# Hyena's filters made beside HGRN's last projections instead of beside the convolutions

## The chip, the cores and the metric

One NeuronCore of a Trainium2 chip runs the whole kernel, alone. The metric is the device time of one execution in microseconds (us), the median of the runs.

## The reference, cut to what matters

Two decoder blocks over 256 tokens of width 1024, all in float32. The change lies in the mixer of the second block, which joins two branches: HGRN (a gated linear recurrence in both directions) and Hyena (a long convolution whose filters a small network makes from positions).

```python
def hybrid_mixer(xn, w_in, ...):
    proj = xn @ w_in                       # q, zf_fwd, zf_bwd, inp, og, hy (3 x 1024), gates (2 x 1024)
    logf = log(lb + (1 - lb) * sigmoid(z)); k = (1 - lb) * sigmoid(-z)      # for z forward and backward
    o = scan(silu(q), k_f, logf_f, inp) + reversed scan(silu(q), k_b, logf_b, inp)
    y_a = (rmsnorm(o) * silu(og)) @ w_branch_a
    x0, x1, v = split(centred_short_conv(hy, conv_w, conv_b))                # width 3, along the tokens
    h_f, h_b = hyena_filters(...)
    y_b = (x0 * bidirectional_fftconv(v * x1, h_f, h_b, bias)) @ w_branch_b
    return (sigmoid(g_a) * y_a + sigmoid(g_b) * y_b) @ w_out

def hyena_filters(L, w1, b1, freq1, w2, b2, freq2, w3, decay_rate):
    z = concat([t, cos(ang), -sin(ang)])                # 256 x 33, constants
    hid = sin(freq1 * (z @ w1 + b1))                    # 256 x 64
    hid = sin(freq2 * (hid @ w2 + b2))                  # 256 x 64
    filt = (hid @ w3) * exp(-t * abs(decay_rate))       # 256 x 2048
    return filt[:, :1024], filt[:, 1024:]
```

The filters depend on weights and constants alone, on nothing that the input has gone through.

## The kernel before, in words

Activations lie transposed in SBUF, 128 channels a partition block, eight blocks of 256 tokens. A weight comes in units of 512 KB (128 x 1024 numbers) over SP's queue into a ring of 3 slots (`SLOTS`). A unit is used in one of two ways. `Whole` (L312) multiplies the float32 as it is: 8 matmuls, recorded as 16 instructions of line L402. `Split` (L334) lets ScalarE round a high part (L338), VectorE (L343) or GpSimd (L349) subtract a low part, into one of 3 buffers (`PARTS`), and multiplies in three passes, 24 matmuls of lines L370 to L372. A unit's product is one step, `Channels`; an "evac" behind it takes the result out of PSUM. `submit` fetches a unit now and plans its product two units later (`AHEAD = 2`).

A step is a small class with a method for each engine. The program is one list of steps, written by Python generators, and each engine goes through the same list in that order (`follow`), doing its own part of each step. Nothing is reordered at run time: an instruction that waits holds up all that stands behind it on its engine. A step with `phases = 3` stands three times in the list, and each time an engine runs to its next `yield`. `filler` generators supply projection units, one at each `next(filler)`, between the phases of other work. `Load` is a small transfer on SP's queue; `Barrier` drains the four compute engines and lets none pass until all have.

`second_mixer` does this, in order:

1. 16 units for the gates' logarithms and keys, with the norm.
2. `hgrn`: two logarithms, four scans, then nine `HgrnLevel`s in `pipeline(..., 2)`: two at a time, on PSUM banks 0 to 3. Each level makes operands (in `zf`, `zb` or in `hg_q2`, `hg_k2`) and the scores of 8 heads in two parts. Beside it the generator `more()` supplies units: q, v, `og`, gate_a and gate_b. It has 42 turns: 8 for q, 1, 8 for v, 1, and 8 each for og, gate_a and gate_b. `hgrn` yields 34 times (1 after the logarithms, 4 scans, 28 phases of levels and an empty turn), and these take 4 + 8 + 29 = 41 turns of `more()`.
3. `finish()`: the one turn left (it plans the product of gate_b's block 5), then `flush(w[32], w[40])`, which plans the products of blocks 6 and 7 and fetches the first two units of the convolutions. Then eight `HgrnHead`s (L2487 to L2494) and a barrier.
4. 24 projections with `ShortConv` behind them (L2796, L2803, L2806, L2810), 14 of their turns beside the `HeadNorm`s of 8 heads, and then 10 turns beside `filters`. A convolution's PSUM bank rotates over three, 4 to 6; it is free when VectorE is done with L2806.
5. `filters`: eight `Load`s (L293), `FilterDecay` (L2584), two `FilterLayer`s of two phases each (L2552 on TensorE, L2559 to L2569 on VectorE, the sine L2574 on ScalarE), and two `FilterTile`s of three phases each (exponential L2604, four matmuls of 512 columns recorded as 8 instructions L2611 into banks 0 to 3, and L2619 to L2625 on VectorE). The first layer's matmul waits for all eight loads; a tile's matmuls wait until VectorE has taken the tile before out of banks 0 to 3 (L2619).
6. A barrier, and then the transforms (`TurnU` L2709, `Transform` L2686), which read the filters.

Of the kernel before, what the change touches and what calls it, by code (L numbers as in the profile page):

```python
# [9 lines left out]
T, D, P = 256, 1024, 128  # L10
NT, KD = T // P, D // P
# [11 lines left out]
HG_H = 8  # L23
# [77 lines left out]
class Signal:  # L101
# [5 lines left out]
    def next(self):  # L107
        self.counted += self.by
        return Mark(self, self.counted)
# [71 lines left out]
def together(main, filler, every):  # L181

    for n, _ in enumerate(main):
        if n % every == 0:
            next(filler, None)
# [2315 lines left out]
def hgrn(c, ctx, s, q, zf, zb, bounded, v, o, finish):  # L2501


    logged = [c.plan(HgrnLogs(c, z[:, :, :], mark)).logged for z, mark in ((zf, bounded[0]), (zb, bounded[1]))]
    s.bf = c.sb("hg_bf", [P, HG_H, T], ctx)
    s.bb = c.sb("hg_bb", [P, HG_H, T], ctx)
    yield
    for back, (z, b) in enumerate(((zf, s.bf), (zb, s.bb))):
        for hd in range(0, HG_H, 4):
            s.scanned = c.plan(HgrnScan(c, z, b, range(hd, hd + 4), back, logged[back])).scanned  # L2510
            yield

    s.places = [(zf, zb), (c.sb("hg_q2", [P, HG_H, T], ctx), c.sb("hg_k2", [P, HG_H, T], ctx))]
    s.at = c.sb("hg_scores", [P, HG_H, NT, P], ctx)
    s.fwd = c.sb("hg_scores_fwd", [P, HG_H, P], ctx)
    s.bwd = c.sb("hg_scores_bwd", [P, HG_H, P], ctx)
    s.cleared = c.plan(HgrnClear(c, s.at[:, :, :, :], bounded[1])).cleared
    s.operands_free, s.kept = [(), ()], [None, None]

    yield from pipeline(c, [lambda u, n=n, m=m: HgrnLevel(c, s, n, m, u) for n, m in enumerate([P] + LEVELS + [0])], 2)  # L2520
    o_free = finish()
    for hd in range(HG_H):
        c.hg_taken = c.plan(HgrnHead(c, s, hd, v, o, o_free)).taken
        yield
# [105 lines left out]
    pass  # L2630


def filters(c, ctx, both):

    f = Filters()
    z = c.sb("filt_z", [EMB, T], ctx)
    w1 = c.sb("filt_w1", [EMB, FILT_H], ctx)
    w2 = c.sb("filt_w2", [FILT_H, FILT_H], ctx)
    f.w3 = c.sb("filt_w3", [FILT_H, 2 * D], ctx)
    vec = c.sb("filt_vec", [FILT_H, 4], ctx)  # L2640
    f.decay = c.sb("filt_decay", [P, 2 * D], ctx)
    f.window = c.sb("filt_window", [P, 2 * D], ctx)
    f.cols = c.sb("filt_cols", [P, 2 * NT], ctx)
    f.hid = c.sb("filt_hid", [FILT_H, T], ctx)
    turns = c.sb("filt_turns", [FILT_H, T], ctx)
    f.came = [c.load(z[:, :], c.dram["filter_z"]), c.load(w1[:, :], c.dram["filt_w1_2"]),
              c.load(w2[:, :], c.dram["filt_w2_2"]), c.load(f.w3[:, :], c.dram["filt_w3_2"]),
              c.load(vec[:, :], c.dram["filt_vec"]),
              c.load(f.decay[:, :], c.dram["filt_decay_2"].partition_broadcast(P)),
              c.load(f.cols[:, 0:NT], c.dram["minus_t"]), c.load(f.cols[:, NT:2 * NT], c.dram["not_first"])]  # L2650
    f.decay_ready = c.plan(FilterDecay(c, f.decay[:, :], f.came)).ready
    ready = f.came
    for n, (w, x) in enumerate(((w1, z), (w2, f.hid))):
        layer = FilterLayer(c, w[:, :], x[:, :], ready, f.hid[:, :], turns[:, :], vec[:, 2 * n:2 * n + 1],
                            vec[:, 2 * n + 1:2 * n + 2])
        ready = list(f.came) + [layer.ready]
        for _ in range(layer.phases):
            c.plan(layer)
            yield
    f.window_free = ()  # L2660
    for i in range(NT):
        tile = FilterTile(c, f, i, layer.ready, both)
        for _ in range(tile.phases):
            c.plan(tile)
            yield
    c.filters_made = tile.made
# [179 lines left out]
def second_mixer(c, h, xn, work, gained, make_norm, following):  # L2846

    w = c.dram["w_in_2"]
    with ExitStack() as ctx:
# [2 lines left out]
        og = c.sb("hg_og", [P, KD, T], ctx)  # L2852
        sga = c.sb("gate_a", [P, KD, T], ctx)
        sgb = c.sb("gate_b", [P, KD, T], ctx)
        o = work
        with ExitStack() as inner:
            q = c.sb("hg_q", [P, HG_H, T], inner)
            zf = c.sb("hg_zf", [P, HG_H, T], inner)
            zb = c.sb("hg_zb", [P, HG_H, T], inner)
            v = c.sb("hg_v", [P, NT, D], inner)  # L2860
            z = [zf[:, n, :] for n in range(KD)] + [zb[:, n, :] for n in range(KD)]
            s = Hgrn()
            s.q = q
            s.kf = c.sb("hg_kf", [P, HG_H, T], inner)
            s.kb = c.sb("hg_kb", [P, HG_H, T], inner)
            k = [s.kf[:, n, :] for n in range(KD)] + [s.kb[:, n, :] for n in range(KD)]
            keys = []

# [45 lines left out]
            filler = in_turns(more())  # L2914

            def finish():
                for _ in filler:
                    pass
                c.whole = False
                c.low_by = "pool"  # L2920
                c.flush(w[32], w[40])
                return xn.whole_free

            for n, _ in enumerate(hgrn(c, inner, s, q, zf, zb, bounded, v, o, finish)):
                for _ in range(4 if n == 0 else 2 if 4 < n < 9 else 1):
                    next(filler, None)
            gated_ready, gates_ready = gates
            c.barrier()
        both = c.sb("filters", [P, NT, 2, D], ctx)
        with ExitStack() as inner:  # L2930
            sq = c.sb("hg_sq", [P, HG_H, T], inner)
            tmps = c.sb("hg_tmp", [P, 2, T], inner)
            x = c.sb("hy_x", [P, T], inner)
            lent = []

            def convolved():
                for n in range(KD):
                    c.channels(w[32 + n], xn, ShortConv(c, n, x0[:, n, :]))
                    yield
                    c.channels(w[40 + n], xn, ShortConv(c, 8 + n, u[:, n, :]))  # L2940
                    yield
                    c.channels(w[48 + n], xn, ShortConv(c, 16 + n, x[:, :], u[:, n, :], lent))
                    yield

            filler = convolved()
            heads, tmps_free = [], [(), ()]

            def head(b, hd):
                norm = HeadNorm(c, o, hd, b, sq, tmps, tmps_free, c.gain("hgrn_norm_g_2"), og, [c.hg_taken, gated_ready])
                heads.append(norm.normed)  # L2950
                return norm

            next(filler)
            next(filler)
            next(filler)
            together(pipeline(c, [lambda b, hd=hd: head(b, hd) for hd in range(HG_H)], 2), filler, 2)
            together(filters(c, inner, both), filler, 1)
            for _ in filler:
                pass
            c.low_by = "vector"  # L2960
            c.flush(c.dram["w_branch_a_2"][0], c.dram["w_branch_a_2"][1])
            u_ready = c.last_conv
            c.barrier()
# [282 lines left out]
```

## Time and profile before

| what | value |
|---|---|
| median of 3 runs | 2531.92 us (2531.15 to 2541.61) |
| the profiled execution's own time | 2539.18 us |
| its span, from first to last instruction | 2537.4 us |
| TensorE busy / VectorE / ScalarE / GpSimd | 94% / 65% / 53% / 31% |
| granted TensorE clock, mean | 0.966 |

Times inside the span are in us from its start. An engine's busy share says little alone here: what counts is who is late at each place. PE is TensorE's matmul row, DVE VectorE, ACT ScalarE, POOL GpSimd, SPq SP's queue of transfers. The clock is given as a share of 2.4 GHz: 1.00 is that, 0.50 is 1.2 GHz.

### The profile page before, as it was taken

How to read it: one execution, taken by the hardware profiler on the slowest of the kernel's cores; microseconds unless marked ns; L12 is line 12 of the kernel's file. 1: busy time of each engine (PE TensorE's matmuls, PEld its weight loads, DVE VectorE, ACT ScalarE, POOL GpSimd, SP SyncE). 2: the span in 40 equal slices, each digit the busy share in tenths (PEclk: the TensorE clock that was granted, in tenths of full speed). 3: DMA queues.
4: the chain of work that ended last, by engine and by line, in shares of the span. 5: the costliest groups of instructions: out<-in, count | busy, mean ns of one | idle time of the engine just before them, and what ended most of it. 6: DMA issues, size and time to landing. Idle time of an engine off the chain costs nothing.

```text
span 2537.4 us, 39066 instructions
## 1 busy us (share of the span) xinstructions
PE 2375.6 (94%) x15354; PEld 2140.5 (84%) x15354; DVE 1660.1 (65%) x3193; ACT 1343.1 (53%) x2494; POOL 775.4 (31%) x404
## 2 busy tenths in 40 slices
PE   6878898999999999998888988899999999999998
PEld 5876788999999888886857976799999999788886
DVE  4564456977777556665667384666977778555555
ACT  3345344468887454444433444244468888444443
POOL 3000002877776000000800152101877777000000
PEclk8888899999999999999999998999999999999999
DMA  5322234555555656664332342254555555565563
GB/s 172 124 95 69 92 100 149 176 176 165 165 164 170 185 191 192 192 192 128 125 116 93 116 148 95 67 165 151 183 175 166 162 164 169 180 189 186 189 187 120
DMA packets 108287, 383.36 MB, mean 151 GB/s; under 512 B 12976, under 2 KB 15841, under 8 KB 107529
## 3 DMA queue, kind: packets, MB, share of 16 engines
q1 hardware_dynamic: 108104, 380.86, 47.3%
q8 instruction: 123, 2.02, 0.3%
q14 instruction: 60, 0.48, 0.1%
HBM read 379.74 MB, written 1.06 MB: 150 GB/s over the span
## 4 chain that ended last, share of the span: by engine, by line
PE 81%; DVE 11%; ACT 4%; DMA 2%; issue 2%; POOL 0%; SPq 0%; DVEq 0%; ACTq 0%; POOLq 0%
PE psum L370 23%; PE psum L372 22%; PE psum L371 22%; PE psum L2021 2%; PE psum L402 2%; DVE weight_parts L343 2%; ACT weight_parts L338 2%; PE psum L607 1%; PE psum L2466 1%; PE psum L2686 1%; PE psum L1457 1%; PE psum L1018 1%; PE psum L1357 0%; DVE hg_tmp L1064 0%; PE psum L2611 0%
## 5 line engine op out<-in xcount | busy, mean ns | idle before, releaser
L349 POOL TENSOR_TENSOR weight_parts<-weight_ring,weight_parts 128x1024 fp32r<-128x1024 f32 x276 | 670.8, 2442 | 506.5 <-ACT weight_parts L338 506.0
L370 PE MATMUL psum<-acts_high,weight_parts 128*128 128x256 f32 x2744 | 794.1, 289 | 23.4 <-DVE weight_parts L343 11.2
L338 ACT ACTIVATE weight_parts<-weight_ring 128x1024 fp32r<-128x1024 f32 x674 | 710.6, 1055 | 150.1 <-PE psum L372 79.2
L372 PE MATMUL psum<-acts_high,weight_parts 128*128 128x256 f32 x2744 | 782.6, 285 | 0.0
L371 PE MATMUL psum<-acts_low,weight_parts 128*128 128x256 f32 x2744 | 782.1, 285 | 0.0
L343 DVE TENSOR_TENSOR weight_parts<-weight_ring,weight_parts 128x1024 fp32r<-128x1024 f32 x398 | 488.4, 1228 | 296.1 <-ACT weight_parts L338 295.5
L370 PEld LDWEIGHTS psum<-acts_high,weight_parts 128*128 128x128 f32 x2744 | 532.1, 194 | 34.6 <-issue 12.5
L371 PEld LDWEIGHTS psum<-acts_low,weight_parts 128*128 128x128 f32 x2744 | 532.4, 194 | 1.4 <-issue 0.5
L372 PEld LDWEIGHTS psum<-acts_high,weight_parts 128*128 128x128 f32 x2744 | 532.4, 194 | 0.0
L370 PE MATMUL psum<-weight_parts,peer_coef 128*128 128x512 f32 x1024 | 405.9, 396 | 4.0 <-issue 3.9
L372 PE MATMUL psum<-weight_parts,peer_coef 128*128 128x512 f32 x1024 | 404.8, 395 | 0.0
L371 PE MATMUL psum<-weight_parts,peer_coef 128*128 128x512 f32 x1024 | 402.8, 393 | 0.0
L2103 ACT ACTIVATE peer_coef<-peer_experts 128x256 fp32r<-128x256 f32 x256 | 106.8, 418 | 356.5 <-PE psum L372 355.4
L370 PEld LDWEIGHTS psum<-weight_parts,peer_coef 128*128 128x128 f32 x1024 | 193.4, 189 | 46.5 <-issue 4.2
L372 PEld LDWEIGHTS psum<-weight_parts,peer_coef 128*128 128x128 f32 x1024 | 193.3, 189 | 45.3
L371 PEld LDWEIGHTS psum<-weight_parts,peer_coef 128*128 128x128 f32 x1024 | 193.2, 189 | 44.3
L2107 DVE TENSOR_TENSOR peer_coef<-peer_experts,peer_coef 128x256 fp32r<-128x256 f32 x256 | 108.5, 425 | 153.6 <-ACT peer_coef L2103 153.6
L2002 ACT ACTIVATE peer_second_keys<-psum,work 128x128 fp32r<-128x128 f32 x512 | 146.2, 371 | 14.9 <-DVE peer_second_keys L1993 13.7
L585 POOL TENSOR_TENSOR work<-h 128x256 f32<-128x256 f32 x32 | 19.4, 614 | 410.7 <-DVE h L569 399.5
L2082 ACT ACTIVATE peer_experts<-psum 128x256 f32<-128x256 f32 (+35 forms) x250 | 78.2, 313 | 121.1 <-PE psum L372 121.0
L1990 DVE TENSOR_TENSOR psum<-psum,work 128x512 f32<-128x512 f32 x128 | 89.2, 697 | 59.7 <-ACT peer_second_keys L2002 58.6
L370 PE MATMUL psum<-acts_spare_high,weight_parts 128*128 128x256 f32 x352 | 103.2, 293 | 16.9 <-DVE weight_parts L343 16.8
(426 smaller groups left out, 3135.4 us busy)
## 6 DMA issues: line engine op xcount, KB each, us to landing
weight_ring<-in_peer_down SPq DMA_DIRECT2D x128, 512.0 KB, 3.6
weight_ring<-in_peer_up SPq DMA_DIRECT2D x128, 512.0 KB, 3.5
weight_ring<-in_peer_u SPq DMA_DIRECT2D x128, 512.0 KB, 3.6
weight_ring<-in_peer_v SPq DMA_DIRECT2D x128, 512.0 KB, 3.5
weight_ring<-in_w_in SPq DMA_DIRECT2D x88, 512.0 KB, 3.6
weight_ring<-in_w_out SPq DMA_DIRECT2D x16, 512.0 KB, 3.6
weight_ring<-in_peer_w_q SPq DMA_DIRECT2D x16, 512.0 KB, 3.6
weight_ring<-in_w_in_v SPq DMA_DIRECT2D x10, 512.0 KB, 3.6
```

The costliest lines, as they stand in the source:

```text
L338: q.e.activation(self.high, self.ring, ACT.Copy).then_inc(*self.rounded.once())
L343: q.e.tensor_tensor(self.low, self.ring, self.high.bitcast(F32), ALU.subtract).then_inc(*self.unit.ready.once())
L349: q.e.tensor_tensor(self.low, self.ring, self.high.bitcast(F32), ALU.subtract).then_inc(*self.unit.ready.once())
L370: q.e.matmul(out, sh, mh, start=first, stop=False)
L371: q.e.matmul(out, sh, ml, start=False, stop=False)
L372: return q.e.matmul(out, sl, mh, start=False, stop=last)
L402: last = q.e.matmul(self.out, w[:, k, :], acts.whole[:, k, :], start=k == 0, stop=k == KD - 1)
L1990: q.e.tensor_tensor(ones, iota, over(x.pairs[:, 1, tokens], P, 2), ALU.is_equal).then_inc(*self.marked.once())
L2002: last = q.e.activation(self.second[:, t, 1, :], self.c.bank(6)[:, P * t:P * t + P], ACT.Copy, bias=0.0, scale=x.gates_low[:, token:token ...
L2082: last = q.e.activation(self.x.experts[:, self.n, n:T], out[:, n:T], ACT.Gelu_apprx_tanh)
L2103: q.e.activation(self.high, self.src, ACT.Copy).then_inc(*self.rounded.once())
L2107: q.e.tensor_tensor(self.low, self.src, self.high.bitcast(F32), ALU.subtract).then_inc(*self.ready.once())
```

## The change

The place in the order changes: `filters` is started in `finish()`, right behind the levels, instead of behind the head norms. Its first turn comes ahead of the last turn of `more()`, its second behind it, and the rest follow at once, ahead of the flush that plans the last two products. The tiles `hg_kf`, `hg_kb`, `hg_q2`, `hg_k2` now lie in a stack of their own (`levels`) which is closed there, and the filters' tiles take that space; so the eight loads wait for the last scores of the last two levels (`s.operands_free`). The result, `both`, lies open from the mixer's start, and `hg_bf`, `hg_bb` are views of it, since the filters are written only when the levels are through. Behind the head norms the call of `filters` goes, and the ten convolution turns that went beside it follow one another.

```diff
-    s.bf = c.sb("hg_bf", [P, HG_H, T], ctx)
-    s.bb = c.sb("hg_bb", [P, HG_H, T], ctx)
...
-    s.at = c.sb("hg_scores", [P, HG_H, NT, P], ctx)
-    s.fwd = c.sb("hg_scores_fwd", [P, HG_H, P], ctx)
-    s.bwd = c.sb("hg_scores_bwd", [P, HG_H, P], ctx)
...
-def filters(c, ctx, both):
+def filters(c, ctx, both, after):
...
-    f.came = [c.load(z[:, :], c.dram["filter_z"]), c.load(w1[:, :], c.dram["filt_w1_2"]),
...
+    f.came = [c.load(out, src, after) for out, src in (
+        (z[:, :], c.dram["filter_z"]), (w1[:, :], c.dram["filt_w1_2"]), (w2[:, :], c.dram["filt_w2_2"]),
+        (f.w3[:, :], c.dram["filt_w3_2"]), (vec[:, :], c.dram["filt_vec"]),
+        (f.decay[:, :], c.dram["filt_decay_2"].partition_broadcast(P)), (f.cols[:, 0:NT], c.dram["minus_t"]),
+        (f.cols[:, NT:2 * NT], c.dram["not_first"]))]
...
+        both = c.sb("filters", [P, NT, 2, D], ctx)
...
-            s.kf = c.sb("hg_kf", [P, HG_H, T], inner)
-            s.kb = c.sb("hg_kb", [P, HG_H, T], inner)
+            s.bf, s.bb = (both[:, i, :, :].rearrange("p a d -> p (a d)").rearrange("p (h t) -> p h t", h=HG_H)
+                          for i in range(NT))
+            s.at = c.sb("hg_scores", [P, HG_H, NT, P], inner)
+            s.fwd = c.sb("hg_scores_fwd", [P, HG_H, P], inner)
+            s.bwd = c.sb("hg_scores_bwd", [P, HG_H, P], inner)
+            levels = inner.enter_context(ExitStack())
+            s.kf = c.sb("hg_kf", [P, HG_H, T], levels)
+            s.kb = c.sb("hg_kb", [P, HG_H, T], levels)
...
             def finish():
+                levels.close()
+                made = filters(c, inner, both, s.operands_free[0] + s.operands_free[1])
+                next(made)
                 for _ in filler:
+                    next(made, None)
+                for _ in made:
                     pass
                 c.whole = False
                 c.low_by = "pool"
                 c.flush(w[32], w[40])
                 return xn.whole_free
 
-            for n, _ in enumerate(hgrn(c, inner, s, q, zf, zb, bounded, v, o, finish)):
+            for n, _ in enumerate(hgrn(c, levels, s, q, zf, zb, bounded, v, o, finish)):
...
-        both = c.sb("filters", [P, NT, 2, D], ctx)
...
             together(pipeline(c, [lambda b, hd=hd: head(b, hd) for hd in range(HG_H)], 2), filler, 2)
-            together(filters(c, inner, both), filler, 1)
             for _ in filler:
                 pass
```

## Rows read from the trace of the kernel before

**Rows 1.** Page, part 1: busy us (share of the span) x instructions.
```profile
PE 2375.6 (94%) x15354; PEld 2140.5 (84%) x15354; DVE 1660.1 (65%) x3193; ACT 1343.1 (53%) x2494; POOL 775.4 (31%) x404
```
**Rows 2.** Stretches, TensorE alone: length, busy (x), granted clock, DMA share, GB/s.
```profile
1454.90:1501.00 46.10, 40.48 (x304) 0.96 0.46 141
1501.00:1559.80 58.80, 50.49 (x308) 0.85 0.34 106
1559.80:1564.20 4.40, 0.04 (x1) 0.84 0.00 0
```
**Rows 3.** TensorE's waits, 1430 to 1640: us in total, times, longest.
```profile
PE psum L2552 <- ACT filt_hid L2574: 4.8, 1, 4.8
PE psum L2709 <- DVEq L816: 4.4, 1, 4.4
```
**Rows 4.** TensorE in order of time: start, us, instruction, [idle before <- releaser].
```profile
1426.33 0.27 PE L2466 MATMUL psum<-hg_q,hg_zb 128*128 128x128 f32 x1
...
1437.32 0.38 PE L402 MATMUL psum<-work,weight_ring 128*128 128x256 f32 x1
...
1447.10 0.27 PE L2487 MATMUL psum<-hg_scores,hg_v 128*128 128x128 f32 x1
...
1502.75 0.61 PE L2552 MATMUL psum<-filt_z,filt_w 33*64 33x256 f32 x2 [1.76 <-DMA filt_cols<-in_not_first]
```
**Rows 5.** SP's queue in order of time: start, us of issuing.
```profile
1434.64 0.33 SPq L334 DMA_DIRECT2D weight_ring<-in_w_in  x1
...
1491.92 0.31 SPq L293 DMA_DIRECT2D filt_z<-in_filter_z  x1
...
1495.66 0.42 SPq L293 DMA_DIRECT2D filt_cols<-in_not_first  x1
```
**Rows 6.** Transfers issued 1486 to 1512: KB, us from issue to landing.
```profile
filt_cols<-in_not_first SPq DMA_DIRECT2D x1, 1.0 KB, 6.9
```
**Rows 7.** The chain that ended last, 1240 to 1640: start, us, what.
```profile
1443.81 3.46 PE psum L402 x16
...
1514.16 1.11 PE psum L2552 x2
...
1524.28 6.26 PE psum L2611 x8
...
1541.55 3.63 PE psum L2611 x8
```
**Rows 8.** ScalarE in order of time.
```profile
1440.97 0.39 ACT L537 ACTIVATE gate_b<-psum 128x256 f32<-128x256 f32 x1 [1.34 <-PE psum L402]
...
1525.08 0.55 ACT L2796 ACTIVATE hy_x<-psum,gains 128x256 f32<-128x256 f32 x1
1525.64 1.28 ACT L2604 ACT_TABLE_LOAD   x1
1526.94 2.00 ACT L2604 ACTIVATE filt_window<-filt_decay,filt_cols 128x2048 f32<-128x2048 f32 x1
```
**Rows 9.** VectorE in order of time.
```profile
1508.66 0.48 DVE L2806 SCALAR_TENSOR_TENSOR hy_x<-psum,gains,hy_x 128x255 f32<-128x255 f32 x1
...
1509.58 0.54 DVE L2559 TENSOR_SCALAR filt_hid<-psum,filt_vec 64x256 f32<-64x256 f32 x1
...
1513.37 0.28 DVE L2569 TENSOR_SCALAR filt_hid<-filt_hid 64x256 f32<-64x256 f32 x1
```
**Rows 10.** Groups by line, 1501 to 1564: xcount, busy us, mean ns, idle before.
```profile
L2619 DVE TENSOR_TENSOR filt_window<-filt_window,psum 128x2048 f32<-128x2048 f32 x2 | 4.6, 2276 | 0.0
...
L2574 ACT ACTIVATE filt_hid<-filt_hid 64x256 f32<-64x256 f32 x2 | 0.8, 416 | 8.8 <-DVE filt_hid L2569 8.8
```
**Rows 11.** Stretches, TensorE alone (columns as in Rows 2).
```profile
1514.10:1518.20 4.10, 4.04 (x16) 0.50 0.00 0
...
1524.20:1535.40 11.20, 11.12 (x31) 0.55 0.32 94
...
1545.10:1559.70 14.60, 14.60 (x121) 1.00 0.30 88
```

More of the change, by code:

```diff
@@ L2645, in filters @@
     turns = c.sb("filt_turns", [FILT_H, T], ctx)
-    f.came = [c.load(z[:, :], c.dram["filter_z"]), c.load(w1[:, :], c.dram["filt_w1_2"]),
[L2647 to L2650, printed above, removed]
+    f.came = [c.load(out, src, after) for out, src in (
[3 more added lines that the diff above has]
+        (f.cols[:, NT:2 * NT], c.dram["not_first"]))]
     f.decay_ready = c.plan(FilterDecay(c, f.decay[:, :], f.came)).ready
```

## The prediction

> **What bounds the kernel now.** The page comes first: TensorE is busy 94% of the span, nobody else over 65% [rows 1]. So an edit pays where it takes away time in which TensorE stands still or runs at the lower clock, and costs where it adds such time. The stretches show both states side by side [rows 2]. In the last stretch of the convolutions (1501.0 to 1559.8) 12 projections of 24 matmuls pass in 58.8 us, with TensorE busy 50.5 us at a mean clock of 0.85. Further on, where the filters' TensorE work is done, five such projections take 14.6 us, 2.9 us each [rows 11]. Twelve at that pace are 34.8 us, so the filters take 24.0 us of TensorE's time there. The list of waits and the order of time name the pieces: 1.8 us for the filters' loads [rows 4], 4.8 us for the first sine [rows 3], 4.1 us of the low clock after it [rows 11], 6.3 and 3.6 us of matmuls for the two tiles [rows 7], and nearly 11 us more of the low clock around the first of them [rows 11]. After the last convolution TensorE waits another 4.4 us for the barrier [rows 2, 3], because VectorE is late there.
>
> The new place has to be read as closely. There, between the levels' last scores (1426.33) and the first head (1447.10), TensorE runs six projections without a gap [rows 4]. Nothing is idle there to be filled on TensorE.
>
> **What the change takes away.** (a) The filters' 24.0 us between 1501.0 and 1559.8. The cover that they leave must be counted. In the fast cadence the third of the 12 projections would start at 1501.0 + 2 x 2.9 = 1506.8. It needs the bank of the third before it, which VectorE, busy with the last two head norms, frees at 1508.66 + 0.48 = 1509.1 [rows 9]. Today that lateness hides behind the filters; then it costs 2.3 us. Bounds: 0, if VectorE gets there sooner, to 4.6, if the low clock follows. I take 2.3. (b) The 4.4 us before the barrier. Without the filters' last instructions ahead of it VectorE needs for the last projection only the evac on ScalarE (0.55 [rows 8]), twice 0.48 [rows 9] and a product of about as much, some 2.1 us. It gains 2.3 us. Together 24.0 - 2.3 + 2.3 = 24.0 us, between 20 and 26.5. The eight transfers and ScalarE's decay that go from here hide behind projections today and gain nothing more.
>
> **What it adds.** The step list says who stands behind whom. `more()` has one turn left when `finish()` starts, so the order on TensorE becomes: gate_b's block 4, the first layer's matmul, block 5, the second layer's matmul, tile 0, tile 1, blocks 6 and 7, the heads. One projection, block 5, lies between two links of the chain; blocks 6 and 7 and the 32 heads' matmuls are ready and stand behind the whole of it. So the filters' latency is laid open almost entirely:
>
> - *The loads.* Their wait for the levels' scores costs nothing: the scores start at 1426.33 [rows 4], and SP gets there when it has issued the transfer at 1434.64 [rows 5]. The last of the eight is issued 3.7 us after the first (1491.92 to 1495.66) and lands 6.9 us on [rows 5, 6]: 1435.0 + 3.7 + 6.9 = 1445.6. TensorE has finished block 4 by 1437.5 (block 5 begins at 1437.32 today [rows 4]) and stands still for about 8 us. Bounds: landing 2 us sooner or later, since two weight units shared the wires today and about as much does then. The weight unit of block 7 is issued 4 us later, behind the loads; its product comes 30 us later, so that is free.
> - *First layer, block 5.* The matmul takes 0.6 [rows 4], to 1446.2. Block 5 takes 3.5 us at the full clock (rows of block 7, [rows 7]); after a stand of 4.8 us the low clock lasted for 4.1 us of work [rows 3, 11], so I take 5.3: 1451.5. The bounds are 3.5 and 6.9.
> - *To the second sine.* VectorE's part of a layer lasts from 1509.58 to 1513.65, 4.1 us, with two convolution instructions of 0.48 in it [rows 9]: 3.1 us net, done by 1449.5, while block 5 runs. But ScalarE has the evac of block 5 ahead of the sine: 0.4 [rows 8], then the table for the sine, 1.3 (as the load at 1525.64 [rows 8]), and the sine, 0.4 [rows 10]: 1453.6. Second layer: matmul 1.1 [rows 7], VectorE 3.1, sine 0.4: 1458.2.
> - *Tile 0.* 6.3 us at the low clock, 3.6 at the full one [rows 7]. It follows a stand of 3.5 us on one of 2, so I take 6.3: 1464.5. The exponential (1.3 and 2.0 [rows 8]) lies beside it. Then L2619, 2.3 us [rows 10], on which tile 1's matmuls wait: 1466.8.
> - *Tile 1.* Between 3.6 and 6.3; I take 5.0: 1471.8. Blocks 6 and 7 start here, at first perhaps at the low clock: 1 us more, with 0 and 2.3 as bounds. Tile 1's work on VectorE ends beside them, before the heads need the banks.
>
> Today block 6 starts at 1437.32 + 3.5 = 1440.8. The place gets longer by 1471.8 + 1.0 - 1440.8 = 32.0 us. With everything at the full clock and the loads 2 us early it is 23; with everything at the low clock and the loads 2 us late, 37.
>
> **A rule weighed.** ScalarE's row shows a table load of 1.28 us between an instruction that ends at 1525.63 and one that starts at 1526.94, with nothing else in the gap [rows 8]. The Trainium skill (ScalarE: Activation LUTs, "What ACT_TABLE_LOAD costs") adds a drain of 1.38 us to every switch of tables. By that rule the sine's switch on the open chain would cost 2.7 instead of 1.3 and the place 33.4 instead of 32.0. The trace does not agree: there is no room for it between the two instructions.
>
> **The sum.** 32.0 - 24.0 = 8 us longer. Against the profiled execution's own 2539.18 that is 2547; it is 7.3 above the median shown, so for the median 2531.9 + 8 = 2540.
>
> **The rivals.**
>
> *The low clock lasts through the whole chain.* One mechanism, in the new place: TensorE gets nothing long enough to do to be granted the full clock between 1441 and block 7. For it: around tile 0 today the clock was low for most of 11.2 us although projections ran [rows 11]; in the new place it has less to do. Against it: after the stand of 4.8 us it was low for only 4.1 us [rows 11]. Price over mine: block 5 6.9 (+1.6), tile 1 6.3 (+1.3), blocks 6 and 7 (+1.3), and the low clock behind the third convolution's wait (+2.3): 14.5 us in sum, 2546. From 12.7 us on it counts as slower, so two or three of these pieces decide.
>
> *The two places cancel.* The full clock returns in each gap and the loads come 2 us early: 23 to 27 against 24, 2532 to 2535. For it: tile 1 took only 3.6 us today [rows 7]. Against it: that tile came after 10 us of unbroken work, and here each piece has a stand of 2 to 8 us ahead.
>
> *The chain is hidden, as the words of the change have it.* If the projections did run beside the filters, only the filters' own matmuls would be added, 0.6 + 0.6 + 3.6 + 3.6 = 8.4 us, against 24.0 saved: 15.6 us faster, 2516. For it: the filters need nothing of TensorE but these 20 matmul records. Against it is the order of the step list: one turn is left, and each engine keeps its order. The 4.8 us before the second layer's matmul [rows 3] show that TensorE does wait with projections ready behind it.
>
> **How the numbers follow.** A measurement of this kernel can tell about 0.5%, 12.7 us, from no change. The sum as forecast 0.50, the low clock's rival 0.30, the two places cancelling 0.16, the hidden chain 0.04. The sum and the cancelling lie within 0.5% (0.66), the low clock beyond it (0.30), the hidden chain is faster (0.04). The range: below, 23 - 26.5 = -3, 2529; above, 37 - 20 = 17 us, 2549, and 3 us more for the spread of the runs: 2552. The hidden chain and half of what lies beyond 2552 stay outside.
>
> **What would show it.** In the profile after: TensorE idle for about 8 us ahead of L2552, released by the load of `not_first`; idle some 2 and 3.5 us ahead of the second L2552 and the first L2611, released by the sine; the first head 30 to 35 us later than 1447.1; a granted clock near 0.5 over most of it; the 12 last convolutions in about 37 us, with one gap of some 2 us; and the barrier's wait at 2 instead of 4.4. The prediction is wrong if projections run between the links of the chain, if the loads land far from 10.6 us after the first issue, or if the last 12 convolutions keep a pace above 3.1 us each.

## The result, and the profile after

After: 2549.97 us (median of 9 runs, 2544.02 to 2555.59). Before, on the same chip: 2535.14 us (9 runs, 2531.09 to 2541.61). The ratio is 1.006, with a 95% interval of 1.0049 to 1.0071, so the change costs 12.4 to 18.0 us. The profiled execution after took 2550.1 us, with a span of 2548.3 and a mean granted clock of 0.963.

The page's first part shows nothing of it. TensorE's busy time stands at 2376.0 against 2375.6 [rows 1]:

```profile
PE 2376.0 (93%) x15354; PEld 2141.6 (84%) x15354; DVE 1663.5 (65%) x3193; ACT 1342.8 (53%) x2494; POOL 770.9 (30%) x404
```

I cut both executions at the same instructions, and take the length of each piece (us):

| piece | before | after | difference |
|---|---|---|---|
| start to the levels' first score | 1294.0 | 1299.9 | +5.9 |
| the levels, first to last score | 134.0 | 135.8 | +1.8 |
| **last score to first head (the new place)** | 18.9 | 55.4 | **+36.5** |
| first head to first evac of a convolution | 11.2 | 11.2 | 0 |
| **first to last evac of the convolutions** | 101.7 | 79.6 | **-22.1** |
| last evac to `TurnU`'s first matmul (barrier) | 4.3 | 2.3 | -2.0 |
| from there to the first transform | 5.5 | 6.3 | +0.8 |
| first transform to the end | 967.8 | 957.8 | -10.0 |

The four pieces that the change can reach from the last score on give +36.5 - 22.1 - 2.0 + 0.8 = +13.2 us. The first and the last piece run the same code in both kernels. Over all the profiled executions of this document the first took 1288 to 1308 us and the last 958 to 968, whatever the kernel. One profile against one can't tell that apart, which is why I compare pieces below and not spans.

The stretches of the new place, TensorE alone (columns as in [rows 2]); the last three are the convolutions and the barrier, which answer to [rows 2]:

```profile
1445.20:1453.20 8.00, 0.01 (x1) 0.81 0.85 270
1453.20:1459.30 6.10, 6.07 (x18) 0.68 0.01 3
1459.30:1465.80 6.50, 0.68 (x3) 0.85 0.46 161
1465.80:1482.70 16.90, 14.37 (x17) 0.50 0.00 1
1482.70:1488.00 5.30, 5.30 (x26) 0.52 0.00 0
1499.10:1543.70 44.60, 38.99 (x304) 1.00 0.38 119
1543.70:1581.90 38.20, 36.30 (x288) 0.96 0.48 152
1581.90:1584.20 2.30, 0.00 (x0) 1.00 0.00 0
```

TensorE stands for 8 us, works for 6, stands again for nearly all of 6.5, and then runs for 22 us (two tiles with one more stand of 2.4 between them, and block 6) at the low level of its clock (0.50 and 0.52, so 1.2 GHz). What it waits for there (us in total, times, longest):

```profile
PE psum L2547 <- DMA filt_cols<-in_not_first: 8.0, 1, 8.0
...
PE psum L2606 <- ACT filt_hid L2569: 3.7, 1, 3.7
...
PE psum L2606 <- DVE filt_window L2614: 2.4, 1, 2.4
PE psum L2705 <- DVEq L816: 2.3, 1, 2.3
PE psum L2547 <- ACT filt_hid L2569: 2.2, 1, 2.2
```

The lines are 5 lower than before: L2547 is a layer's matmul (before L2552), L2606 a tile's (L2611), L2569 the sine, L2614 the first product of a tile. Four of the rows are the chain's own links, 16.3 us; the fifth is the barrier's wait, 2.3 instead of 4.4 [rows 3]. The chain that ended last runs through the same instructions:

```profile
1446.54 6.45 DMA filt_cols<-in_not_first
1453.23 1.08 PE psum L2547 x2
1454.31 5.04 PE psum L402 x16
1459.77 1.28 ACT L2569
1461.07 0.42 ACT filt_hid L2569
1461.54 0.66 PE psum L2547 x2
...
1465.88 7.21 PE psum L2606 x8
1473.18 2.30 DVE filt_window L2614
1475.53 7.19 PE psum L2606 x8
```

One projection, block 5 (L402), lies between two links; all the others come ahead of the chain or behind it. The eight instructions of a tile took 7.21 and 7.19 us here, 6.26 and 3.63 before [rows 7].

### The profile page after: what moved, and what is told of

Same layout as the page of the kernel before. It is cut to its first block, busy times and chain, and to the rows that moved or that the text cites. A ratio compares the mean times of both kernels' runs of the same rounds, so it can differ in the third digit from the quotient of the medians.

```text
span 2548.3 us, 39060 instructions
## 1 busy us (share of the span) xinstructions
PE 2376.0 (93%) x15354; PEld 2141.6 (84%) x15354; DVE 1663.5 (65%) x3193; ACT 1342.8 (53%) x2494; POOL 770.9 (30%) x404
## 4 chain that ended last, share of the span: by engine, by line
PE 77%; DVE 15%; ACT 4%; DMA 2%; issue 2%; SPq 0%; POOL 0%; DVEq 0%; ACTq 0%; POOLq 0%
PE psum L370 22%; PE psum L372 21%; PE psum L371 21%; PE psum L2021 2%; PE psum L402 2%; DVE weight_parts L343 2%; ACT weight_parts L338 1%; PE psum L607 1%; PE psum L2466 1%; PE psum L2682 1%; PE psum L1457 1%; PE psum L1018 1%; DVE peer_experts L1887 1%; DVE peer_experts L1879 1%; DVE peer_experts L1881 1%
## 5 line engine op out<-in xcount | busy, mean ns | idle before, releaser
L338 ACT ACTIVATE weight_parts<-weight_ring 128x1024 fp32r<-128x1024 f32 x674 | 710.8, 1055 | 143.0 <-PE psum L372 81.6
```

The lines of the kernel that those rows point to most:

```text
L338: q.e.activation(self.high, self.ring, ACT.Copy).then_inc(*self.rounded.once())
```

## The experiments

All times are medians with the ratio to the kernel before on the same chip. "The place" is the piece from last score to first head: 18.9 us before, 55.4 after. `e1` to `e4` were measured beside a before of 2537.23, `e5` to `e7` of 2535.18, `e8` and `e9` of 2536.5, `e10` and `e11` of 2541.59. Where the chain ends right ahead of the heads, the low clock behind it falls on the heads, which the place leaves out: from first head to first evac it is 13.4 us in e4, 13.1 in e7, 12.9 in e9 and 12.2 in e8, against 11.2 before and after.

| | median | ratio [95%] | levels | place | convolutions |
|---|---|---|---|---|---|
| e1 loads early | 2542.73 | 1.0025 [1.0006, 1.0045] | 138.5 | 45.7 | 79.6 |
| e2 none | 2508.78 | 0.9878 [0.9854, 0.9902] | 135.9 | 18.9 | 79.0 |
| e3 warm | 2537.02 | 1.0002 [0.9989, 1.0016] | 132.9 | 44.5 | 79.6 |
| e4 blocks first | 2552.09 | 1.0057 [1.0032, 1.0081] | 137.8 | 54.4 | 78.9 |
| e5 woven | 2541.04 | 1.0024 [1.0003, 1.0045] | 143.6 | 38.2 | 78.9 |
| e6 spread | 2549.57 | 1.0052 [1.0026, 1.0079] | 134.2 | 18.9 | 118.2 |
| e7 fetch first | 2545.03 | 1.0035 [1.0016, 1.0053] | 137.8 | 51.7 | 79.0 |
| e8 woven behind | 2528.70 | 0.9980 [0.9960, 1.0000] | 138.5 | 32.1 | 78.9 |
| e9 order alone | 2535.20 | 0.9994 [0.9975, 1.0013] | 138.8 | 35.3 | 79.1 |
| e10 woven around | 2521.33 | 0.9919 [0.9890, 0.9947] | 137.8 | 29.6 | 79.0 |
| e11 burst | 2526.56 | 0.9947 [0.9923, 0.9971] | 139.7 | 29.6 | 79.2 |

**e2_none.** The filters are left out altogether; the transforms read whatever lies in `both`. What do they cost in each place?

```diff
-                made = filters(c, inner, both, s.operands_free[0] + s.operands_free[1])
-                next(made)
                 for _ in filler:
-                    next(made, None)
-                for _ in made:
                     pass
+                c.filters_made = None
```

> The changed kernel with the filters left out altogether (no loads, layers, tiles; the transforms read what HGRN left in that space, so the output isn't the reference's). It measures both sides of the sum at once. Theory 1: the place shrinks from 44.2 us later than before to 7.7 later in the profiled pair, so 36.5 us go: 2550 - 36.5 = 2513, 22 below the kernel before. Rival (the convolutions ran slowly before for another reason than the filters beside them): less than 15 below the kernel before, 2520 or more.

The place is 18.9 us, as before, and the convolutions take 79.0. So after's 36.5 us in the place are the filters' whole, and before they cost 101.7 - 79.0 = 22.7 between the convolutions and 2.1 at the barrier, near the 24.0 that I had read off. By the pieces this kernel is 24.6 us shorter than before, by the medians 28.4 (interval 24.9 to 37.0). No edit accounts for the rest; it stays open.

**e1_loads_early.** The eight loads are planned ahead of gate_a's units, into tiles laid out before the levels' or views of `x0` and `u`, which are free there. Nothing else moves.

```diff
...
+                load_filters(c, f, [c.last_kept])
                 for n in range(KD):
                     c.channels(w[56 + n], xn, Keep(sga[:, n, :]))
...
-                made = filters(c, inner, both, s.operands_free[0] + s.operands_free[1])
+                made = filters(c, inner, both, f)
```

> The changed kernel, with the filters' eight loads issued in the middle of HGRN's levels, behind og's projections (w3 lies in the space of hy_x0, decay in that of hy_u, both unused until the convolutions). Theory 1 (the place costs the sum of the chain's latencies, laid open by the order of the steps): the stand of 8.0 us ahead of the first layer's matmul goes, and with it the low clock in block 5 (5.1 instead of 3.5 us): 9.6 us less than the changed kernel, 2540. The tiles stay at 7.2 us each. Rival (something else of the place binds, such as ScalarE behind block 5, and the stand only moves on): the second layer's matmul comes no earlier than 4 us before, 2546 or more.

The place is 9.7 us shorter. The stand of 8.0 us is gone, and with it the low clock of the first layer and block 5; the other links and the low clock from the first tile to block 6 are as they were. TensorE's waits, and the whole stretch from the first layer to block 7:

```profile
PE psum L2606 <- ACT filt_hid L2569: 3.7, 1, 3.7
PE psum L2606 <- DVE filt_window L2614: 2.5, 1, 2.5
PE psum L2547 <- ACT filt_hid L2569: 2.3, 1, 2.3
```
```profile
1447.40:1484.00 36.60, 28.12 (x79) 0.67 0.12 43
```

**e3_warm.** After, with 34 spare matmuls (17, 4, 8 and 5) into a bank of no use ahead of the chain's links. They add work and change nothing else, so they separate the clock from the waits.

```diff
+                c.plan(Dummies(c, 17))
                 next(made)
                 for _ in filler:
                     next(made, None)
+                c.plan(Dummies(c, 4))
+                next(made)
+                next(made)
+                c.plan(Dummies(c, 8))
...
+                c.plan(Dummies(c, 5))
```

> The changed kernel with 34 matmuls more, of the ones by a constant tile into PSUM bank 7, read by nobody: 17 ahead of the first layer's matmul, 4 ahead of the second, 8 ahead of tile 0, 5 ahead of tile 1, about as long at the full clock (0.43 us each) as TensorE stands still in each place. It takes the low clock away and leaves every latency. Theory 1: block 5 loses 1.6 us, the tiles 3.6 each, block 6 2.4 and the first layer 0.5: 11 us less than the changed kernel, 2539, still above the kernel before. Rival (the low clock is the main cost of the place): over 20 us less, below 2530.

The clock is 1.00 through the whole stretch, and the place is 10.9 us shorter with more work in it. That prices the low clock:

```profile
1442.50:1477.90 35.40, 33.83 (x146) 1.00 0.29 93
```

The kernel is back at the time of before (1.0002). By the pieces: 36.5 - 10.9 for the place, -22.1 for the convolutions, -2.0 and +0.3 around the barrier give +1.8.

**e4_blocks_first.** Blocks 5, 6 and 7 go ahead of the filters; only the loads are planned before them.

```diff
+    yield
     f.decay_ready = c.plan(FilterDecay(c, f.decay[:, :], f.came)).ready
...
                 for _ in filler:
-                    next(made, None)
-                for _ in made:
                     pass
                 c.whole = False
                 c.low_by = "pool"
                 c.flush(w[32], w[40])
+                for _ in made:
+                    pass
```

> The changed kernel, with the loads issued where they are, but blocks 5, 6 and 7 of gate_b planned ahead of the first layer, so that their 10 us lie beside the landing of the loads; the chain then stands alone, ahead of the heads. Theory 1: the stand of 8.0 us is covered and ScalarE has no evac ahead of the sine; the chain still costs 0.6 + 3.6 + 1.1 + 3.6 + 7.2 + 2.4 + 7.2 us, the heads wait 2.4 us more for tile 1's L2614 and start at the low clock: 6 to 8 us less than the changed kernel, 2543. Rival (projections between the links matter more than the landing): no gain, 2550.

A miss by 9 us: the place is 54.4. The loads stand ahead of block 7's weight unit on SP's queue, and TensorE now waits for that unit instead of for `not_first`; and with no projection left between them the links are as bare as before. The filters' last work also moved in front of the heads (L2487):

```profile
PE psum L402 <- DMA weight_ring<-in_w_in: 4.6, 1, 4.6
PE psum L2547 <- ACT filt_hid L2569: 3.7, 1, 3.7
PE psum L2606 <- ACT filt_hid L2569: 3.7, 1, 3.7
PE psum L2487 <- DVE filt_window L2614: 2.5, 1, 2.5
```

**e7_fetch_first.** Like e4, but the loads too are planned behind the fetch of block 7's weight unit.

```diff
+    yield
     f.decay_ready = c.plan(FilterDecay(c, f.decay[:, :], f.came)).ready
...
-                next(made)
                 for _ in filler:
-                    next(made, None)
-                for _ in made:
                     pass
+                next(made)
                 c.whole = False
                 c.low_by = "pool"
                 c.flush(w[32], w[40])
+                for _ in made:
+                    pass
```

> e4_blocks_first with the weights of block 7 fetched ahead of the filters' eight loads instead of behind them. In e4_blocks_first TensorE stood 4.6 us for them, and block 7 then took 6.0 us at the low clock. Theory 1: both go, 7 us less than e4_blocks_first, the place 47 instead of 54.4 us, 2545. Rival (the covered landing of the filters' loads is now the wait): the place no shorter than 52.

The time came out as expected, but the place is 51.7 and not 47. The stand of 8.0 is gone, and 7.8 us came at the second layer. ScalarE's rounding of a convolution's weight unit (L338) is ahead of the sine on its queue and waits 6.44 us for that unit. It lands late: the two units issued behind the loads took 7.2 us from issue to landing (median), against 3.7 for the units around the place before:

```profile
PE psum L2547 <- ACT filt_hid L2569: 7.8, 1, 7.8
```
```profile
1446.57 1.06 ACT L338 ACTIVATE weight_parts<-weight_ring 128x1024 fp32r<-128x1024 f32 x1 [6.44 <-DMA weight_ring<-in_w_in]
```

After, e4 and e7 together: a burst of loads at the time of use costs 4 to 8 us wherever it is put (8.0 in after, 4.6 in e4, 7.8 instead of e4's 3.7 at the second layer in e7). e1, whose loads are issued by 1373.7, 74 us ahead of the first layer, is rid of it.

**e5_woven.** e1, with both layers beside the last phases of the levels, the tiles among the last blocks. The layers use PSUM bank 7, which the levels leave free.

```diff
-        self.bias, self.freq, self.b = bias, freq, 3
+        self.bias, self.freq, self.b = bias, freq, 7
...
+                if n == 29:
+                    made = filters(c, inner, both, f)
+                if 29 < n < 34:
+                    next(made)
...
+                next(made)
+                next(made)
+                next(made)
                 c.whole = False
                 c.low_by = "pool"
-                c.flush(w[32], w[40])
+                c.prepared.append(c.fetch(w[32]))
+                c.work_off()
+                for _ in made:
+                    pass
+                c.flush(w[40])
```

> The filters in the new place, woven so that a projection stands between every two links: loads early as in e1_loads_early; the two layers on PSUM bank 7, their four turns beside the last level's phases (blocks 2 to 4 between them); tile 0 ahead of block 5, tile 1 ahead of block 6, block 7 and the heads behind. Theory 1: only the filters' own matmuls stay on TensorE, 0.6 + 0.6 + 3.6 + 3.6 = 8.4 us at the full clock and a little waiting: the place is 18.9 + 9 to 12 instead of 55.4 us, the convolutions stay as short as in the changed kernel; 2537 - 24 + 11 = 2524, about 13 below the kernel before. Rival (ScalarE, with two more table switches among gate_b's evacs, binds instead): place over 40, 2535 or more.

A miss by 17 us. The place fell to 38.2, but the levels rose to 143.6. Projections did lie between the links; now each link stood behind something else on its own engine. TensorE's waits, and what ScalarE did:

```profile
PE psum L2606 <- ACT filt_hid L2569: 4.7, 1, 4.7
PE psum L2466 <- DVE hg_scores L2435: 2.6, 1, 2.6
```
```profile
1455.42 1.06 ACT L338 ACTIVATE weight_parts<-weight_ring 128x1024 fp32r<-128x1024 f32 x1 [3.20 <-DMA weight_ring<-in_w_in]
```

A level's scores waited for a copy behind the filters' work on VectorE, and the tile's matmuls for a sine behind a weight unit that had not landed.

**e6_spread.** The other side: the kernel before, with its filters not behind but among the head norms, where the convolutions run anyway.

```diff
+    yield
     f.decay_ready = c.plan(FilterDecay(c, f.decay[:, :], f.came)).ready
...
-            together(pipeline(c, [lambda b, hd=hd: head(b, hd) for hd in range(HG_H)], 2), filler, 2)
-            together(filters(c, inner, both), filler, 1)
+            made = filters(c, inner, both)
+            next(made)
+            for n, _ in enumerate(pipeline(c, [lambda b, hd=hd: head(b, hd) for hd in range(HG_H)], 2)):
+                if n % 2 == 0:
+                    next(filler, None)
+                if n in (10, 13, 16, 19):
+                    next(made)
+            for n, _ in enumerate(made):
+                next(filler, None)
+                if n in (0, 3):
+                    next(filler, None)
```

> The kernel before, the filters at their old place, but with the loads at the stage's start, the four turns of the layers beside the head norms, three of their phases apart, and the tiles' six turns beside eight of the last ten convolutions' turns. Theory 1 (what the filters cost there was latency with too few projections between the links, and the place as such is not at fault): the waits of 1.8, 4.8 and 1.7 us and half of the low clock go, 12 us below the kernel before, 2525. Rival (VectorE, which carries the head norms, passes the layers' 6 us on to TensorE): 5 or less below, 2532.

A miss by 25 us: the convolutions take 118.2 instead of 101.7. There VectorE is the late one, and the filters' instructions are put in its way: a head norm's sum waits 7.9 us, since its square stands behind the first sine on ScalarE, and the sine waits for VectorE. The loads at the head of the stage delay the weights: the two units issued right behind them took 8.0 us to land (median), and ScalarE waits 7.52 us:

```profile
PE psum L1050 <- ACT hg_sq L1040: 9.2, 3, 7.9
PE psum L2611 <- ACT filt_hid L2574: 6.9, 1, 6.9
PE psum L370 <- POOL weight_parts L349: 6.2, 2, 5.7
```
```profile
1466.56 1.06 ACT L338 ACTIVATE weight_parts<-weight_ring 128x1024 fp32r<-128x1024 f32 x1 [7.52 <-DMA weight_ring<-in_w_in]
```

**e9_order_alone** and **e8_woven_behind.** e1's loads; behind the levels the blocks 5, 6 and 7 are dealt out, one between two links (`work_off` plans a product that has been fetched). e8 adds three things: gate_b's sigmoid is taken off the blocks' evacs and done later in one instruction, so ScalarE changes its table less; the heads use banks 4 to 7, so that they needn't wait for the filters' last product; and `flush(w[32])` goes ahead of the tiles' last part. The edit of e9:

```diff
                 made = filters(c, inner, both, f)
                 next(made)
+                next(made)
                 for _ in filler:
-                    next(made, None)
+                    pass
+                next(made)
+                next(made)
+                c.work_off()
+                next(made)
+                c.work_off()
                 for _ in made:
                     pass
```

and what e8 has besides:

```diff
-        self.b = hd % 4
+        self.b = (7, 4, 5, 6)[hd % 4]
...
-                    c.channels(w[64 + n], xn, Keep(sgb[:, n, :], ACT.Sigmoid))
+                    c.channels(w[64 + n], xn, Keep(sgb[:, n, :]))
...
-                c.flush(w[32], w[40])
+                c.flush(w[32])
+                for _ in made:
+                    pass
+                c.flush(w[40])
...
+        gate_b_ready = c.plan(Activate(c, sgb[:, :, :], ACT.Sigmoid, gate_b_kept)).ready
```

> e1_loads_early with nothing changed but the order in finish(): both turns of the first layer, block 5, both of the second, block 6, tile 0's matmuls, block 7, then the rest. e5_woven moved three things at once and put links behind weights that were still landing and behind VectorE's parts of the last level; here the levels are left alone and no weight is fetched between the links. Theory 1: TensorE's row from block 4 to the first head is 0.6 + 3.5 + 0.6 + 3.1 + 0.5 + 3.6 + 3.5 + 3.6 us and 2.6 for the heads' wait on tile 1's L2614, 21.6 where the kernel before has 10: place 30 instead of e1_loads_early's 45.7 us, 2526, 11 below the kernel before. Rival (a chain between short projections stays open, since ScalarE serves evac, sine and tables in one row): place 38 or more, 2533.

> e9_order_alone, and beside it tile 0's part on VectorE and tile 1's matmuls behind block 7 as there, but the heads on PSUM banks 7, 4, 5 and 6 instead of 0 to 3, so that they don't wait for tile 1, and gate_b kept plain out of PSUM, with one sigmoid over all of it much later, so that no table is switched between the links. Theory 1: the heads' wait of 2.6 us goes: place 28, 2523, 14 below the kernel before. Rival (the wait only moves on to the barrier behind the heads, or the later sigmoid costs as much): equal to e9_order_alone within 1 us of the sum of the stretches.

e9 came 9 us above its expectation, with a place of 35.3 instead of 30; e8 with 32.1 instead of 28. Of the waits, 6.9 us are left in e9:

```profile
PE psum L2487 <- DVE filt_window L2614: 3.8, 1, 3.8
PE psum L2547 <- ACT filt_hid L2569: 2.5, 1, 2.5
PE psum L2606 <- ACT filt_hid L2569: 0.6, 1, 0.6
```

The order is the larger step, 45.7 to 35.3; e8's three edits give 3.2 more together, and 0.8 in the heads. They were not run apart.

**e10_woven_around** and **e11_burst.** The first layer goes into the levels' last phase (turn 33), where the levels' own work is over, the second among the blocks; gate_b's sigmoid is late, as in e8, and the loads go out one by one beside the units of `og`. e11 is e10 with the loads in one burst ahead of gate_a's units, as in e1.

```diff
+                if n == 33:
+                    made = filters(c, inner, both, f)
+                    next(made)
+                    next(made)
+                    c.work_off()
+                    next(made)
+                    next(made)
...
                 for _ in filler:
-                    next(made, None)
+                    pass
+                next(made)
+                c.work_off()
+                next(made)
+                next(made)
+                next(made)
+                c.work_off()
```

and from e10 to e11:

```diff
                     c.channels(w[24 + n], xn, Keep(og[:, n, :]))
-                    if n == 0:
-                        loads = load_filters(c, f, [c.last_kept])
-                    next(loads)
                     yield
+                load_filters(c, f, [c.last_kept])
                 for n in range(KD):
                     c.channels(w[56 + n], xn, Keep(sga[:, n, :]))
```

> The links of the chain one projection further forward than in e8_woven_behind, each with its successor one projection away and no link behind a weight that still lands: first layer (both turns), block 4, second layer (both turns), block 5, tile 0's matmuls, block 6, tile 0's rest and tile 1's matmuls, block 7, tile 1's rest, heads on banks 0 to 3 as before; the fetch of block 6's weights comes behind the second layer. The eight loads go out one at a time beside og's eight projections. gate_b plain, with the late sigmoid. Theory 1: the filters' own 8.4 us on TensorE and nothing else: place 27 to 28 us (18.9 before, 32.1 in e8_woven_behind), 14 us below the kernel before by the stretches, 2522. Rival (another queue takes over again: VectorE's or ScalarE's weight parts): place over 31.

> e10_woven_around with its eight loads in one burst behind og's projections, as in e1, e8 and e9, whose levels took 138.5 to 138.8 us where they took 134.0 before. If the burst of 1.5 MB makes the weights of gate_a late, the levels take 138 us here and 134 in e10_woven_around, and 4 us stand between the two; if those 4 us are the clock's own spread between executions, the two kernels agree within 2 us.

e10 beats both kernels: 0.9919 of before, 20 us less (interval 13 to 28). The whole place runs at the full clock, and the links' waits sum to under 1 us:

```profile
1428.90:1455.30 26.40, 25.59 (x118) 1.00 0.25 80
```
```profile
PE psum L2547 <- ACT filt_hid L2569: 0.7, 1, 0.7
...
PE psum L2487 <- DVE filt_window L2614: 0.2, 1, 0.2
```

Its place is 29.6 us (27 to 28 were expected), 10.7 above before; that is the filters' own matmuls, 8.4 us, and 2 us. By the pieces from the last score on it is 14 us shorter than before, with the levels' +3.8 it is 10; the medians say 13 to 28, so they are kinder than the one profile. The place of e11 is the same 29.6. Neither outcome of its expectation came: its levels took 139.7 us against 137.8, and the medians stand 5 us apart. The two ratios' intervals overlap: that the burst costs anything there is not shown.

## Why the prediction came out as it did

The forecast was +8 us, 2540; what came was about +15, 2550. That lies inside the range but outside the forecast's own "within 0.5%". The first rival, the low clock that lasts, came nearer with its +14.5 (2546; both sums were counted from the 2531.92 shown, and before's nine runs have 2535.14). Step by step, with after's times brought to before's scale (this execution reached the place 7.7 us later):

- **The order, and the chain laid open: right.** TensorE's queue shows it as forecast, and the rival that hides the chain fell.
- **The loads: right.** A stand of 8.0 us for `not_first`, as forecast. e1 gives it back, 9.7 us in the place.
- **First layer, block 5, second sine: right.** Block 5 ended within 0.2 us of the forecast and tile 0 began within 0.1. The rival had block 5 at 6.9; it took 5.04. The clock had fallen during the stand of 8.0 us and came back inside block 5, at 1457.0; it was at 0.50 again from the stand ahead of tile 0 until the end of block 6:

```profile
1450.20:1457.00 6.80, 3.77 (x9) 0.50 0.36 141
1457.00:1463.80 6.80, 2.98 (x13) 1.00 0.44 154
1464.00:1487.70 23.70, 19.37 (x39) 0.50 0.00 1
```

- **Tile 0: 6.3 forecast, 7.2 measured.** The row of 6.26 [rows 7] was taken for a tile at the low clock; it was one in which the clock fell on the way. Before, TensorE passed the tile's first us at 0.99 and the rest at 0.50 (the 0.55 over the stretch [rows 11] holds both):

```profile
1524.28:1525.28 1.00, 1.00 (x3) 0.99 0.00 0
1525.30:1530.54 5.24, 5.24 (x8) 0.50 0.33 97
```

  A tile all at 0.50 takes 7.2, twice the 3.63 of full speed.
- **Tile 1: 5.0 forecast, 7.2 measured.** Here the sum failed most, by 2.2 us. I took a value inside bounds of 3.6 and 6.3, and the upper one was too low as well. Behind the stand of 3.7 the clock stayed at 0.50 through both tiles, with 7.2 us of unbroken work on either side of the stand of 2.4.
- **Block 6: +1.0 forecast, +2.4 measured.** Its 24 matmuls passed at a mean of 0.52.
- These three make 0.9 + 2.2 + 1.4 = 4.5 us, and the place came out at +36.5 instead of +32.0. e3 shows the cause: with the clock held at 1.00 the same place is 10.9 us shorter, and the sum had 6.9 us of low clock in it (1.8 in block 5, 2.7 and 1.4 in the tiles, 1.0 in block 6). The step that was mis-sized is the price of the low clock in the tiles and block 6, whose mechanism I had and whose size I split with its rival. The upper bound was added up wrongly too: with everything at the low clock and the loads 2 us late the terms give 38.2, not 37.
- **The gain: 24.0 forecast, 23.3 measured; the sum is near, its parts came otherwise.** Convolutions -22.1, barrier -2.0, transforms +0.8. Of the 22.1, 1.5 came ahead of the filters' old place (46.1 to 44.6 us at clocks of 0.96 [rows 2] and 1.00), which the sum did not have. The last 12 convolutions took 38.2 us where it had 37.1. That is 3.18 us each, just past the 3.1 which the prediction had set as a sign of being wrong. The wait of 2.3 for the third product's bank did not come. In its place the first product of the stretch waited 1.89 us for GpSimd's low part and then ran at the low clock; the stretch ended 3.4 us above the fast pace:

```profile
1545.58 0.42 PE L370 MATMUL psum<-acts_high,weight_parts 128*128 128x256 f32 x1 [1.89 <-POOL weight_parts L349]
```

- **The table rule of the Trainium skill (ScalarE: Activation LUTs, "What ACT_TABLE_LOAD costs"): not borne out, as forecast.** ScalarE's rows of after show the load and the sine behind it with 0.02 us between them, as before; there is no drain of 1.38 us. The measurement decides here: a switch costs 1.3 us.

```profile
1459.37 0.38 ACT L537 ACTIVATE gate_b<-psum 128x256 f32<-128x256 f32 x1 [4.37 <-PE psum L402]
1459.77 1.28 ACT L2569 ACT_TABLE_LOAD   x1
1461.07 0.42 ACT L2569 ACTIVATE filt_hid<-filt_hid 64x256 f32<-64x256 f32 x1
```

The pieces give +13.2, the medians +12.4 to +18.0. That both are past +8 is shown; the 2 us between them are not explained.

The levels took 134 us in before and e6, 133 to 136 in after, e2 and e3, 137.8 to 138.8 in e1, e4, e7, e8, e9 and e10, 139.7 in e11 and 143.6 in e5. They go with the granted clock inside them: 0.95, 0.94, 0.93, 0.91 and 0.92 in that order. e4 and e7 have their loads late and stand with the slower ones, so the traces do not show that early loads slow the levels. Why the clock differs there is open.

## What to carry to other kernels

In these runs a dependent chain of short pieces was hidden only where the in-order list itself had independent work between every two links, on every engine that the chain passes (e10). Moving it "beside" such work left it bare, and then the stands were paid twice, as waits and as the low clock that came with them (here 16 us and 11 us). Ahead of such a move, look at each engine's queue for what stands before the link, above all an instruction that waits for a weight still on its way; and issue the chain's loads a stage early.

## What the runs showed of the hardware that was not expected

- A tile's eight matmul instructions took 7.2 us at a granted clock of 0.50 and 3.63 at 1.00 [rows 7]; 34 spare matmuls, which hold the clock, made the place shorter by 10.9 us.
- Unbroken work did not keep the clock up or bring it back at once. Before, it fell 1 us into tile 0, behind a stand of 1.7 us, and stayed at 0.50 for the rest of the tile. After, it stayed at 0.50 from 1464.0 to 1487.7 although TensorE was busy for 19.37 of these 23.7 us, the last 12 of them without a gap. Why is open.
- VectorE slows beside GpSimd. In e9 the same sum of the filters, two inputs in SBUF, took 1.23 us while GpSimd was idle and 3.27 when GpSimd was making low parts beside it; the next of the kind, which began at 1470.12, after GpSimd's end at 1469.10, took 1.21. The first fence is VectorE's, the second GpSimd's:

```profile
1458.56 1.23 DVE L2619 TENSOR_TENSOR filters<-filt_window 128x1024 f32<-128x1024 f32 x1
...
1466.93 3.27 DVE L2619 TENSOR_TENSOR filters<-filt_window 128x1024 f32<-128x1024 f32 x1
```
```profile
1463.98 5.12 POOL L349 TENSOR_TENSOR weight_parts<-weight_ring,weight_parts 128x1024 fp32r<-128x1024 f32 x2 [204.35 <-ACT weight_parts L338]
```

The Trainium skill (SBUF — State Buffer, "Who interferes with whom") says that a VectorE instruction with two SBUF inputs contends with a GpSimd instruction that reads SBUF; the trace agrees.
- Eight loads issued in a burst delayed the weights behind them. The two units behind them took 7.2 us to land in e7 and 8.0 in e6 (medians), against 3.7 around the place before.
- The same code, from the start to the levels' first score, took 1288 to 1308 us in thirteen profiled executions. A difference of a few us between two spans says nothing of a change.
